# The last stage of a mixture-of-experts layer: expert outputs gathered in two parts, and the first weighting on ScalarE

## The chip, the core and the metric

The kernel runs on one core of a Trainium2 chip. The metric is the device time of one execution in microseconds (us). A profile of one execution gives the times of single instructions and transfers. Engines are called PE (TensorE), DVE (VectorE), ACT (ScalarE), POOL (GpSimd) and SP (SyncE).

## The reference

One layer serves two sequences, 128 prompt tokens and 256 sample tokens of width 2048, all float32. It has a token mixer (gated linear attention beside long convolutions) and then a mixture of experts. The change touches only the latter:

```python
def _moe(h, l, p):
    ...
    grp = jnp.argmax(lg, axis=-1)                      # one of 4 groups
    top_v, top_i = lax.top_k(jax.nn.softmax(le_sel, axis=-1), TOP_K_IN_GROUP)   # 2 of its 4 experts
    ids = grp[:, None] * EXP_PER_GROUP + top_i
    gates = jnp.sum(jax.nn.one_hot(ids, N_EXPERTS, dtype=f32) * (p_grp[:, None] * top_v)[..., None], axis=1)
    for e in range(N_EXPERTS):
        he = jax.nn.silu(t @ p['w_exp_gate'][l, e]) * (t @ p['w_exp_up'][l, e])
        out = out + gates[:, e:e + 1] * (he @ p['w_exp_down'][l, e]).astype(f32)

# in _layer, after it:
    x = x + gt2 * _rmsnorm(y, p['g_post_ffn'][l])
```

Each of the 384 tokens has two experts out of 16, so there are 768 pairs of a token and an expert. With the inputs used 44 of them are expert 15's, and none of the counts but two is above 64.

## The kernel before

The mixer and the router fill the time up to about 1250 us. The router ranks the 768 pairs and gives each a slot: an expert's pairs lie together, padded to blocks of 64 slots. `slot_i[:, r, t]` holds the slots of choice `r` of the 128 tokens of tile `t` (three tiles), `wpair` the two weights of each token. `tab_i` is a small table of numbers that all engines read into registers: the count of blocks `nblk`, and for each expert the number of the block after its last (`tab_i[..., MAXB + 2 + e]`, from `r_end`). The experts run in order, so the last block is the last expert's.

**The loop over blocks.** PE runs `expert_block(e, b)` (L706 to L739) once for each block. In this order it

- multiplies the block's token rows by the gate and up weights (L716, 64 matmuls),
- waits at L720 for `x_gathered >= b * 16 + 32`, and then turns the *next* block's rows into columns (`turn_rows`, L687, 16 transposes),
- waits for `he`, which ACT (silu, L1099) and DVE (product, L1488) make, turns it (L726),
- multiplies by the down weights (L736, 32 matmuls).

ACT and DVE evict the result (L1103, L1493) and ACT stores it to `y_slots` in DRAM with two DMAs (L1108, semaphore `y_stored`, 32 a block on top of 1).

**Weights.** SP loads six 2 MB pieces for each expert into nine places of 16 KB a partition (`MOE_SLOTS`), in turn; a load waits until PE has used the place (L813). The semaphore of place `i` is `w{i}`. The last piece is load number 95 and goes to place 5. Places 6, 7 and 8 take their last loads for expert 14, as loads 87 to 89.

**POOL.** Its queue is one list in program order. First its loop over `nblk + 1` fetches (L910 to L918): each waits until PE has turned the rows before it, loads 64 token numbers into `idx_i` (L913), waits for them and gathers those rows of `h_rows` into `hg` (L916; it adds 16 to `x_gathered`). PE's transposes of block 17 wait for the 19th fetch, number 18, though no block follows: all of its indices are beyond the table, and such rows are skipped. After its loop POOL waits for all stores (L920) and issues six gathers (L924), one for each tile and choice, 128 rows of 8 KB each.

**The tail.** DVE combines tile by tile (`combine`, L1497): the first row times its weight (L1501), plus the second row times its weight (L1504), times the gate of the modulation (L1510). ACT makes the sum of squares (L959) and the root (L965), DVE adds the residual (L1515), and SP stores the tile (L819).

Of the kernel before, what the change touches and what calls it, by code (L numbers as in the profile page):

```python
# [13 lines left out]
F32 = mybir.dt.float32  # L14
# [6 lines left out]
P = 128  # L21
# [22 lines left out]
RING = 3  # L44
BLK = 64
MAXB = NE + (2 * TOK - 2) // BLK
MAGIC = 1.5 * 2.0 ** 23
TWO_PI_HI = 6.28125
TWO_PI_LO = 2 * math.pi - TWO_PI_HI
# [84 lines left out]
def build(nc, T):  # L134

    ctx = ExitStack()
    with ctx:
        def sb(name, shape, dt=F32):
            return ctx.enter_context(nc.sbuf_tensor("s_" + name, shape, dt))
# [29 lines left out]
        tok_i = sb("tok_i", [P, NT], I32)  # L169
        tab_i = sb("tab_i", [P, MAXB + 2 + NE], I32)  # L170
        idx_i = sb("idx_i", [BLK, 1], I32)
        ident, tri = base[:, 0:P], base[:, P:2 * P]
        sel = base[:, 2 * P:4 * P].rearrange("p (c m) -> p c m", c=2)
        ps = ctx.enter_context(nc.psum_tensor("ps", [P, 8, NCOL], F32))
# [83 lines left out]
        he = at(AT_MOD + D, DE, rows=BLK)  # L258
        sg = at(AT_GAIN + 512, DE, rows=BLK)
        ysl = at(AT_GAIN + 1024, 2, NCOL)  # L260
        yga = [[region((2 * t + r) * D, D) for r in range(2)] for t in range(NT)]


        h_dram = nc.dram_tensor("h_rows", [TOK, D], F32).ap()
        y_dram = nc.dram_tensor("y_slots", [NE * BLK + 3 * DEC, D], F32).ap()
        tok_dram = nc.dram_tensor("tok_of_slot", [(MAXB + 1) * BLK, 1], I32).ap()

        x_rows = [T["x_prompt"][0], T["x_sample"][0, 0:P], T["x_sample"][0, P:2 * P]]
# [555 lines left out]
        def _(pool):  # L824
# [82 lines left out]
            pool.wait_ge(S("tables_ready"), 1)  # L907

            nblk = pool.value_load(tab_i[0:1, MAXB:MAXB + 1], min_val=NE, max_val=MAXB)
            with pool.Fori(0, nblk + 1) as b:  # L910
                pool.wait_ge(S("x_turns"), b * 2 + 1)
                pool.nop(nofuse=True)
                pool.dma_start(idx_i[:, :], tok_dram[bass.ds(b * BLK, BLK), :]).then_inc(S("idx_in"), 16)  # L913
                pool.wait_ge(S("idx_in"), b * 16 + 16)
                pool.nop(nofuse=True)
                pool.indirect_dma_start(out=hg, out_offset=None, in_=h_dram,  # L916
                                        in_offset=bass.IndirectOffsetOnAxis(ap=idx_i[:, :], axis=0),
                                        bounds_check=TOK - 1, oob_is_err=False).then_inc(S("x_gathered"), 16)  # L918

            pool.wait_ge(S("y_stored"), nblk * 32 + 1)  # L920
            pool.nop(nofuse=True)
            for t in range(NT):
                for r in range(2):
                    pool.indirect_dma_start(out=yga[t][r], out_offset=None, in_=y_dram,  # L924
                                            in_offset=bass.IndirectOffsetOnAxis(ap=slot_i[:, r, t:t + 1], axis=0)
                                            ).then_inc(S(f"y_gathered{t}{r}"), 16)


        @block.scalar
        def _(act):  # L930
# [165 lines left out]
            with act.Fori(0, nblk) as b:  # L1096
                act.wait_ge(S("used3"), b + 2)
                act.wait_ge(S("he_ready"), b + 1)
                A(sg, ps[BLK:2 * BLK, 0, :], ACT.Silu).then_inc(S("sg_ready"), 1)  # L1099
                turned(b * 2 + 4)  # L1100
                act.wait_ge(S("used5"), b + 2)
                act.wait_ge(S("y_stored"), b * 32 + 1)
                A(ysl[:, 0, :], ps[:, 4, :], ACT.Copy).then_inc(S("y_read_act"), 1)  # L1103
                act.wait_ge(S("y_read_act"), b + 2)
                act.wait_ge(S("y_read_dve"), b + 2)
                rows = y_dram[bass.ds(b * BLK, BLK), :].rearrange("r (a c n) -> r a c n", a=2, c=2)
                for c in range(2):
                    act.dma_start(rows[:, :, c, :], ysl[c * BLK:(c + 1) * BLK, :, :]).then_inc(S("y_stored"), 16)  # L1108
            for t in range(NT):
                act.wait_ge(S("y_added"), t + 1)  # L1110
                squares(yga[t][0], y_sb[:, 0, :], 32 + t)
                roots(32 + t, 1, D)
# [4 lines left out]
        def _(dve):  # L1117
# [283 lines left out]
            def step(ins, sem=None):  # L1401
                v.op(ins, sem)
                v.sync()
# [72 lines left out]
                                  ALU.add))  # L1476
            step(ve.tensor_scalar(r_tab[:, 0:MAXB], r_tab[:, 0:MAXB], float(NE - 1), None, ALU.min))
            v.op(ve.tensor_copy(tab_i[:, :], r_tab), S("tables_ready"))


            dve.wait_ge(S("tables_ready"), 1)
# [14 lines left out]

            def combine(t):  # L1497

                dve.wait_ge(S(f"y_gathered{t}0"), 16)
                y0, y1 = yga[t]  # L1500
                v.op(ve.tensor_scalar(y0, y0, wpair[:, 0, t:t + 1], None, ALU.mult))  # L1501
                v.sync()
                dve.wait_ge(S(f"y_gathered{t}1"), 16)
                v.op(ve.scalar_tensor_tensor(out=y0, in0=y1, scalar=wpair[:, 1, t:t + 1], in1=y0, op0=ALU.mult,  # L1504
                                             op1=ALU.add), S("y_added"))
                v.sync()
                if t < 2:
                    for j in range(4):
                        read(dve, f"gate1{j}{t}")
                v.op(ve.tensor_tensor(y1.rearrange("p (j n) -> p j n", j=4), y0.rearrange("p (j n) -> p j n", j=4),  # L1510
                                      ps[:, 4 * COND[t]:4 * COND[t] + 4, :], ALU.mult))
# [36 lines left out]
```

## Time and profile before

| | |
|---|---|
| median of 3 runs | 1816.5 us (1803.3 to 1820.69) |
| the profiled execution | 1822.51 us, of which the span is 1820.8 us |
| busy: PE, DVE, ACT, POOL | 1563.7, 376.1, 229.1, 82.4 us |
| DMA, mean over the span | 230 GB/s |
| the last 60 us: PE's last block's first matmul | 1748.14 us |
| PE's last down-projection matmul ends | 1777.7 us |
| first of the six gathers issued | 1783.38 us |
| DVE's last instruction ends | 1816.4 us |

How to read it: the engines' shares are means over stages with different limits. The change lies in the last 60 us, so what counts there is what each step waits for. Beside a wait it matters what stands behind the waiting instruction in the same engine's list. All DMAs that POOL issues go through one queue, those of SP and of ACT through one each; the page gives them as q0, q1 and q10.

### The profile page before, as it was taken

How to read it: one execution, taken by the hardware profiler on the slowest of the kernel's cores; microseconds unless marked ns; L12 is line 12 of the kernel's file. 1: busy time of each engine (PE TensorE's matmuls, PEld its weight loads, DVE VectorE, ACT ScalarE, POOL GpSimd, SP SyncE). 2: the span in 40 equal slices, each digit the busy share in tenths (PEclk: the TensorE clock that was granted, in tenths of full speed). 3: DMA queues.
4: the chain of work that ended last, by engine and by line, in shares of the span. 5: the costliest groups of instructions: out<-in, count | busy, mean ns of one | idle time of the engine just before them, and what ended most of it. 6: DMA issues, size and time to landing. Idle time of an engine off the chain costs nothing.

```text
span 1820.8 us, 14118 instructions
## 1 busy us (share of the span) xinstructions
PE 1563.7 (86%) x5712; PEld 714.3 (39%) x5712; DVE 376.1 (21%) x716; ACT 229.1 (13%) x370; POOL 82.4 (5%) x122
## 2 busy tenths in 40 slices
PE   3689989989999699999998999784998987899781
PEld 0244434434555354545454444362333332333230
DVE  0122300000213344445362000421000000000005
ACT  1203200100000101101012000210110110011011
POOL 4000000000000000000001000001000000000001
PEclk8889999999898699999898999756998998899995
DMA  9964544554615523424122221462999999999975
GB/s 350 421 254 180 218 170 171 231 190 180 236 46 220 191 98 139 162 93 145 46 93 73 93 93 51 180 271 80 404 404 359 404 401 399 411 393 399 395 330 219
DMA packets 67821, 418.30 MB, mean 230 GB/s; under 512 B 6827, under 2 KB 7068, under 8 KB 46036
## 3 DMA queue, kind: packets, MB, share of 16 engines
q1 hardware_dynamic: 55124, 375.69, 52.0%
q0 software_dynamic: 6496, 29.08, 4.9%
q10 hardware_dynamic: 6144, 12.71, 1.9%
q8 instruction: 44, 0.72, 0.2%
q14 instruction: 13, 0.11, 0.0%
HBM read 404.33 MB, written 23.08 MB: 235 GB/s over the span
## 4 chain that ended last, share of the span: by engine, by line
PE 70%; DMA 18%; DVE 5%; issue 4%; ACT 2%; POOL 0%; SPq 0%; ACTq 0%; POOLq 0%; DVEq 0%
PE ps L449 19%; PE ps L452 19%; PE ps L716 10%; DMA s_mem<-in_w_exp_gate 10%; PE ps L736 6%; DMA s_mem<-in_w_ada 4%; PE ps L378 3%; PE ps L554 3%; PE ps L614 2%; DMA s_mem<-in_w_in 2%; PE ps L566 2%; PE ps L420 1%; PE ps L522 1%; PE ps L503 1%; DMA s_mem<-in_hy_w 1%
## 5 line engine op out<-in xcount | busy, mean ns | idle before, releaser
L452 PE MATMUL ps<-s_mem 128*128 128x512 f32 x768 | 340.6, 605 | 14.9 <-DMA s_mem<-in_w_in 14.9
L449 PE MATMUL ps<-s_mem 128*128 128x384 f32 x1024 | 341.7, 495 | 5.6 <-DMA s_mem<-in_w_in 4.5
L716 PE MATMUL ps<-s_mem 128*64 128x512 f32 x1152 | 266.1, 620 | 34.1 <-DMA s_mem<-in_w_exp_gate 33.4
L449 PEld LDWEIGHTS ps<-s_mem 128*128 128x128 f32 x1024 | 197.5, 194 | 152.3 <-issue 16.0
L452 PEld LDWEIGHTS ps<-s_mem 128*128 128x128 f32 x768 | 147.8, 194 | 207.0 <-issue 189.4
L716 PEld LDWEIGHTS ps<-s_mem 128*64 128x64 f32 x1152 | 88.7, 143 | 208.4 <-issue 207.6
L736 PE MATMUL ps<-s_mem 128*64 128x512 f32 x576 | 148.4, 675 | 9.3 <-DVE s_mem L1490 9.3
L378 PE MATMUL ps<-s_mem,s_sT 128*32 128x512 f32 x768 | 103.3, 672 | 29.2 <-DMA s_mem<-in_w_ada 29.2
L736 PEld LDWEIGHTS ps<-s_mem 128*64 128x64 f32 x576 | 44.6, 154 | 99.9 <-issue 87.9
L1488 DVE TENSOR_TENSOR s_mem<-s_mem,ps 64x512 f32<-64x512 f32 x18 | 12.2, 679 | 338.8 <-ACT s_mem L1099 338.8
L984 ACT ACTIVATE s_mem<-ps 128x512 f32<-128x512 f32 (+1 forms) x69 | 39.0, 582 | 315.0 <-PE ps L452 187.7
L554 PE MATMUL ps<-s_mem 128*128 128x512 f32 x160 | 71.0, 599 | 3.1 <-ACT s_mem L984 3.1
L378 PEld LDWEIGHTS ps<-s_mem,s_sT 128*32 128x32 f32 x768 | 22.5, 117 | 99.2 <-issue 56.3
L1099 ACT ACT_TABLE_LOAD x18 | 23.1, 1283 | 287.2 <-PE ps L716 287.2
L687 PE MATMUL ps<-s_base,s_mem 64*128 64x64 f32 x304 | 37.5, 276 | 22.8 <-DMA s_mem<-h_rows,s_idx_i 22.8
L687 PEld LDWEIGHTS ps<-s_base,s_mem 64*128 64x128 f32 x304 | 34.9, 200 | 37.5 <-DMA s_mem<-h_rows,s_idx_i 22.9
L1036 ACT ACTIVATE s_mem<-ps,s_colB 128x384 f32<-128x384 f32 x24 | 16.1, 670 | 257.8 <-PE ps L449 257.8
L1159 DVE TENSOR_TENSOR s_mem<-s_mem,ps 128x512 f32<-128x512 f32 x6 | 4.1, 683 | 206.3 <-PE ps L378 206.3
L554 PEld LDWEIGHTS ps<-s_mem 128*128 128x128 f32 x160 | 29.5, 190 | 41.9 <-issue 35.0
L566 PE MATMUL ps<-s_mem,s_hdn 64*128 64x512 f32 x48 | 31.5, 806 | 14.8 <-DMA s_mem<-in_hy_w 12.7
L1493 DVE COPY s_mem<-ps 128x512 f32<-128x512 f32 x18 | 12.5, 692 | 152.0 <-PE ps L736 152.0
L1312 DVE RECIPROCAL s_mem<-ps 128x512 f32<-128x512 f32 x8 | 26.3, 3326 | 79.4 <-PE ps L575 79.4
(221 smaller groups left out, 964.3 us busy)
## 6 DMA issues: line engine op xcount, KB each, us to landing
s_mem<-in_w_ada SPq DMA_DIRECT2D x48, 2048.0 KB, 11.1
s_mem<-in_w_exp_up SPq DMA_DIRECT2D x32, 2048.0 KB, 30.7
s_mem<-in_w_exp_gate SPq DMA_DIRECT2D x32, 2048.0 KB, 26.6
s_mem<-in_w_exp_down SPq DMA_DIRECT2D x32, 2048.0 KB, 29.9
s_mem<-in_w_in SPq DMA_DIRECT2D x24, 2048.0 KB, 11.3
s_mem<-in_w_out SPq DMA_DIRECT2D x8, 2048.0 KB, 8.1
y_slots<-s_mem ACTq DMA_DIRECT2D x36, 256.0 KB, 12.2
h_rows<-s_mem SPq DMA_DIRECT2D x3, 1024.0 KB, 6.0
```

The source lines that it names most:

```text
L378: m = mm(ps[32 * j:32 * j + 32, bank, :], sT[:, k, :], w[:, n, :], start=(k == 0), stop=(k == KT - 1), skip_group_check=True)
L449: m = mm(ps[:, banks[m_], 0:TOK], v[:, k, m_ * P:(m_ + 1) * P], hT[:, kk, :], start=(kk == 0), stop=(kk == KT - 1))
L452: m = mm(ps[:, banks[m_], :], hT[:, kk, m_ * P:(m_ + 1) * P], v[:, k, :], start=(kk == 0), stop=(kk == KT - 1))
L554: m = mm(ps[:, bank, :], dft[:, FWD[t, rows], :], src(t), start=(t == tiles[0]), stop=(t == tiles[-1]))
L566: mm(ps[:, 4 + d, :], hdn[:, t * P:(t + 1) * P], w3[:, d, :], start=True, stop=True).then_inc(filled(f"f{ho}{t}{d}"), 1)
L614: m = mm(ps[:, t, :], dft[:, INV[r, t], :], Yb[:, r, :], start=(r == rows[0]), stop=(r == rows[-1]))
L687: m = tr(ps[:, 2 + i, q * BLK:(q + 1) * BLK], hg[:, k:D:KT], ident[0:BLK, 0:BLK])
L716: m = mm(ps[half, 0, :], hgT[:, kh * 8 + k, :], weights(e, 2 * kh + which)[:, k, :], start=(kh + k == 0), stop=(kh * 8 + k == KT - 1), ski ...
L736: m = mm(ps[half, 4 + n // 2, :], heT[:, 2 * kh + k, :], weights(e, 4 + kh)[:, k, n * NCOL:(n + 1) * NCOL], start=(kh + k == 0), stop=(kh ...
L984: a.op(A(dst, ps[:, b, 0:n], func), freed("act", key))
L1099: A(sg, ps[BLK:2 * BLK, 0, :], ACT.Silu).then_inc(S("sg_ready"), 1)
L1312: v.op(ve.reciprocal(Gs[:, 3 + s, :], ps[:, b, :]), freed("dve", f"norm{ho}{s}"))
```

## The change

Three things change.

- **POOL gathers twice.** Its loop of fetches is split at `last`, the end of expert 14's blocks, read from `tab_i` into a register. After fetch `last` it waits until the stores of all blocks before the last expert's are done, until the split tables are written, and until the last weight load has landed (`w5`). Then it issues six gathers with `early_i`. Then come the remaining fetches, `last + 1` to `nblk`. Then it waits for the early gathers and for all stores, and issues six gathers with `late_i`. The index tables are made so that the early ones skip the last expert's rows and the late ones skip all others (a skipped row's index is beyond the bound).
- **The destination of the rows** is places 6, 7 and 8 of the weights, in place of the region at the start of the arena.
- **The first weighting** (row one times its weight) moves from DVE to ACT, as `weigh(t)`, one tile ahead.

DVE makes the two index tables from `slot_i` in eight small operations.

```diff
@@ -44,6 +44,8 @@
 RING = 3
 BLK = 64
 MAXB = NE + (2 * TOK - 2) // BLK
+Y_ROWS = NE * BLK + 3 * DEC
+NO_ROW = 4096
 MAGIC = 1.5 * 2.0 ** 23
 TWO_PI_HI = 6.28125
 TWO_PI_LO = 2 * math.pi - TWO_PI_HI
@@ -169,6 +171,9 @@
         tok_i = sb("tok_i", [P, NT], I32)
         tab_i = sb("tab_i", [P, MAXB + 2 + NE], I32)
         idx_i = sb("idx_i", [BLK, 1], I32)
+        early_i = sb("early_i", [P, 2 * NT], I32)
+        late_i = sb("late_i", [P, 2 * NT], I32)
+        split = sb("split", [P, 3 * 2 * NT + 1])
         ident, tri = base[:, 0:P], base[:, P:2 * P]
         sel = base[:, 2 * P:4 * P].rearrange("p (c m) -> p c m", c=2)
         ps = ctx.enter_context(nc.psum_tensor("ps", [P, 8, NCOL], F32))
@@ -258,11 +263,12 @@
         he = at(AT_MOD + D, DE, rows=BLK)
         sg = at(AT_GAIN + 512, DE, rows=BLK)
         ysl = at(AT_GAIN + 1024, 2, NCOL)
-        yga = [[region((2 * t + r) * D, D) for r in range(2)] for t in range(NT)]
+        yga_at = [MOE_SLOTS[i] + o for i in (6, 7, 8) for o in (0, D)]
+        yga = [[at(yga_at[2 * t + r], D) for r in range(2)] for t in range(NT)]


         h_dram = nc.dram_tensor("h_rows", [TOK, D], F32).ap()
-        y_dram = nc.dram_tensor("y_slots", [NE * BLK + 3 * DEC, D], F32).ap()
+        y_dram = nc.dram_tensor("y_slots", [Y_ROWS, D], F32).ap()
         tok_dram = nc.dram_tensor("tok_of_slot", [(MAXB + 1) * BLK, 1], I32).ap()

         x_rows = [T["x_prompt"][0], T["x_sample"][0, 0:P], T["x_sample"][0, P:2 * P]]
@@ -907,7 +913,9 @@
             pool.wait_ge(S("tables_ready"), 1)

             nblk = pool.value_load(tab_i[0:1, MAXB:MAXB + 1], min_val=NE, max_val=MAXB)
-            with pool.Fori(0, nblk + 1) as b:
+            last = pool.value_load(tab_i[0:1, MAXB + 2 + NE - 2:MAXB + 2 + NE - 1], min_val=1, max_val=MAXB)
+
+            def fetch(b):
                 pool.wait_ge(S("x_turns"), b * 2 + 1)
                 pool.nop(nofuse=True)
                 pool.dma_start(idx_i[:, :], tok_dram[bass.ds(b * BLK, BLK), :]).then_inc(S("idx_in"), 16)
@@ -917,13 +925,31 @@
                                         in_offset=bass.IndirectOffsetOnAxis(ap=idx_i[:, :], axis=0),
                                         bounds_check=TOK - 1, oob_is_err=False).then_inc(S("x_gathered"), 16)

+            def gather_y(index):
+                for t in range(NT):
+                    for r in range(2):
+                        at_ = r * NT + t
+                        pool.indirect_dma_start(out=yga[t][r], out_offset=None, in_=y_dram,
+                                                in_offset=bass.IndirectOffsetOnAxis(ap=index[:, at_:at_ + 1], axis=0),
+                                                bounds_check=Y_ROWS - 1, oob_is_err=False
+                                                ).then_inc(S(f"y_gathered{t}{r}"), 16)
+
+            with pool.Fori(0, last + 1) as b:
+                fetch(b)
+            pool.wait_ge(S("y_stored"), last * 32 + 1)
+            pool.nop(nofuse=True)
+            pool.wait_ge(S("slots_split"), 1)
+            i = LOADS_A_EXPERT * NE - 1
+            pool.wait_ge(S(f"w{i % len(MOE_SLOTS)}"), 16 * (i // len(MOE_SLOTS) + 1))
+            gather_y(early_i)
+            with pool.Fori(last + 1, nblk + 1) as b:
+                fetch(b)
+            for t in range(NT):
+                for r in range(2):
+                    pool.wait_ge(S(f"y_gathered{t}{r}"), 16)
             pool.wait_ge(S("y_stored"), nblk * 32 + 1)
             pool.nop(nofuse=True)
-            for t in range(NT):
-                for r in range(2):
-                    pool.indirect_dma_start(out=yga[t][r], out_offset=None, in_=y_dram,
-                                            in_offset=bass.IndirectOffsetOnAxis(ap=slot_i[:, r, t:t + 1], axis=0)
-                                            ).then_inc(S(f"y_gathered{t}{r}"), 16)
+            gather_y(late_i)


         @block.scalar
@@ -1106,7 +1132,14 @@
                 rows = y_dram[bass.ds(b * BLK, BLK), :].rearrange("r (a c n) -> r a c n", a=2, c=2)
                 for c in range(2):
                     act.dma_start(rows[:, :, c, :], ysl[c * BLK:(c + 1) * BLK, :, :]).then_inc(S("y_stored"), 16)
+            def weigh(t):
+                act.wait_ge(S(f"y_gathered{t}0"), 32)
+                a.op(A(yga[t][0], yga[t][0], ACT.Copy, scale=wpair[:, 0, t:t + 1]), S("y_weighed"))
+
+            weigh(0)
             for t in range(NT):
+                if t + 1 < NT:
+                    weigh(t + 1)
                 act.wait_ge(S("y_added"), t + 1)
                 squares(yga[t][0], y_sb[:, 0, :], 32 + t)
                 roots(32 + t, 1, D)
@@ -1476,6 +1509,16 @@
                                   ALU.add))
             step(ve.tensor_scalar(r_tab[:, 0:MAXB], r_tab[:, 0:MAXB], float(NE - 1), None, ALU.min))
             v.op(ve.tensor_copy(tab_i[:, :], r_tab), S("tables_ready"))
+            n = 2 * NT
+            slot_f, is_late, moved, cut = split[:, 0:n], split[:, n:2 * n], split[:, 2 * n:3 * n], split[:, 3 * n:3 * n + 1]
+            v.op(ve.tensor_scalar(cut, r_end[:, NE - 2:NE - 1], float(BLK), None, ALU.mult))
+            step(ve.tensor_copy(slot_f, slot_i.rearrange("p r t -> p (r t)")))
+            step(ve.tensor_scalar(is_late, slot_f, cut, float(NO_ROW), ALU.is_ge, ALU.mult))
+            step(ve.tensor_tensor(moved, slot_f, is_late, ALU.add))
+            step(ve.tensor_copy(early_i[:, :], moved))
+            step(ve.tensor_tensor(moved, slot_f, is_late, ALU.subtract))
+            step(ve.tensor_scalar(moved, moved, float(NO_ROW), None, ALU.add))
+            step(ve.tensor_copy(late_i[:, :], moved), S("slots_split"))


             dve.wait_ge(S("tables_ready"), 1)
@@ -1496,11 +1539,9 @@

             def combine(t):

-                dve.wait_ge(S(f"y_gathered{t}0"), 16)
+                dve.wait_ge(S("y_weighed"), t + 1)
                 y0, y1 = yga[t]
-                v.op(ve.tensor_scalar(y0, y0, wpair[:, 0, t:t + 1], None, ALU.mult))
-                v.sync()
-                dve.wait_ge(S(f"y_gathered{t}1"), 16)
+                dve.wait_ge(S(f"y_gathered{t}1"), 32)
                 v.op(ve.scalar_tensor_tensor(out=y0, in0=y1, scalar=wpair[:, 1, t:t + 1], in1=y0, op0=ALU.mult,
                                              op1=ALU.add), S("y_added"))
                 v.sync()
```

On POOL, from its loop of fetches to the end, the list before is as follows (an ISA row is a register, branch or wait instruction; "waits" names semaphores):

```order
L910 UNCONDITIONAL_BRANCH
L910 ISA
L913 ISA [waits x_turns]
L913 DMA s_idx_i<-tok_of_slot 64x1
L914 ISA
L916 DMA s_mem<-h_rows,s_idx_i 64x2048 [waits idx_in]
L910 ISA
L910 COMPARE_AND_BRANCH
L920 ISA
L924 DMA s_mem<-y_slots,s_slot_i 128x2048 [waits y_stored]
L924 DMA s_mem<-y_slots,s_slot_i 128x2048 x5
```

And with the change, from the end of its first loop of fetches:

```order
L937 COMPARE_AND_BRANCH
L939 ISA
L932 DMA s_mem<-y_slots,s_early_i 128x2048 [waits y_stored,w5,slots_split]
L932 DMA s_mem<-y_slots,s_early_i 128x2048 x5
L945 ISA
L945 UNCONDITIONAL_BRANCH
L945 ISA
L921 ISA [waits x_turns]
L921 DMA s_idx_i<-tok_of_slot 64x1
L922 ISA
L924 DMA s_mem<-h_rows,s_idx_i 64x2048 [waits idx_in]
```

The last fetches now stand behind three waits and six gathers. On PE nothing has moved; in `expert_block` it has, with the change as before:

```order
L726 ISA
L693 MATMUL ps<-s_base,s_mem 128x64 [waits x_gathered]
L693 MATMUL ps<-s_base,s_mem 128x64 x15
L729 REGISTER_ALU
L732 MATMUL ps<-s_base,s_mem 128x64 [waits he_ready]
L732 MATMUL ps<-s_base,s_mem 128x64 x3
L742 MATMUL ps<-s_mem 64x512 [waits y_read_dve,w4,y_read_act,he_turned]
```

These are the transposes of the next block's rows, those of `he`, and the first down matmuls, with the wait for the fetch ahead of all three. In the tail ACT now begins with

```order
L1137 ACTIVATE s_mem<-s_mem,s_wpair 128x2048 [waits y_gathered00]
L1137 ACTIVATE s_mem<-s_mem,s_wpair 128x2048 [waits y_gathered10]
L985 ACTIVATE s_mem,s_stat<-s_mem 128x2048 [waits y_weighed,y_added]
L991 ACT_TABLE_LOAD
L991 ACTIVATE s_stat<-s_stat 128x1 [waits act_step]
L1137 ACTIVATE s_mem<-s_mem,s_wpair 128x2048 [waits y_gathered20]
```

where only the squares, the table load and the root stood; the number of table loads is the same.

## Rows read from the trace of the kernel before

**Rows 1.** the page's DMA issues: engine, op, count, KB, us to landing.

```profile
y_slots<-s_mem ACTq DMA_DIRECT2D x36, 256.0 KB, 12.2
```

**Rows 2.** the chain of waits from 1600 us: start, us, what.

```profile
1768.96 8.81 PE ps L736 x32
...
1779.51 3.08 DMA y_slots<-s_mem
...
1792.54 2.36 DVE s_mem L1504
...
1797.21 1.21 DVE s_mem L1501
```

**Rows 3.** timeline of POOL: start, us, instruction [idle before <-releaser].

```profile
1248.40 0.57 POOL L913 DMA_DIRECT2D s_idx_i<-tok_of_slot  x1 [3.91 <-issue]
...
1251.48 0.97 POOL L916 DMA_INDIRECT s_mem<-h_rows,s_idx_i  x1 [2.50 <-DMA s_idx_i<-tok_of_slot]
...
1746.19 0.95 POOL L916 DMA_INDIRECT s_mem<-h_rows,s_idx_i  x1 [5.88 <-DMA s_idx_i<-tok_of_slot]
...
1783.38 0.98 POOL L924 DMA_INDIRECT s_mem<-y_slots,s_slot_i  x1 [36.24 <-DMA y_slots<-s_mem]
...
1789.66 1.55 POOL L924 DMA_INDIRECT s_mem<-y_slots,s_slot_i  x1 [0.31 <-issue]
```

**Rows 4.** instructions on h_rows, 1738 to 1760: fetch 18.

```profile
L916 POOL DMA_INDIRECT s_mem<-h_rows,s_idx_i x1: 949/949/949, 1746.2 to 1746.2; - x1
...
DMA to landing us min/median/max: 7.5/7.5/7.5
```

**Rows 5.** timeline of the last block, 1762 to 1784.

```profile
1764.86 1.97 PE L687 MATMUL ps<-s_base,s_mem 64*128 64x64 f32 x16
...
1767.78 0.66 PE L726 MATMUL ps<-s_base,s_mem 64*128 64x64 f32 x4 [0.95 <-DVE s_mem L1488]
...
1768.48 0.42 DVE L1490 COPY s_mem<-ps 128x256 f32<-128x256 f32 x1 [0.84 <-PE ps L726]
```

**Rows 6.** instructions on y_slots, 1748 to 1760: block 16's stores.

```profile
L1108 ACTq DMA_DIRECT2D y_slots<-s_mem x2: 543/544/544, 1749.4 to 1750.1; - x2
...
DMA to landing us min/median/max: 9.8/12.7/15.7
```

**Rows 7.** instructions on in_w_exp_down, 1735 to 1752: last load.

```profile
L788 SPq DMA_DIRECT2D s_mem<-in_w_exp_down x1: 327/327/327, 1737.5 to 1737.5; - x1
...
DMA to landing us min/median/max: 30.6/30.6/30.6
```

**Rows 8.** source line 924, the six gathers: issue to landing.

```profile
DMA to landing us min/median/max: 5.6/9.6/12.6
```

**Rows 9.** on s_idx_i, 1247 to 1253: index load (min), gather (max).

```profile
DMA to landing us min/median/max: 2.2/3.5/4.7
```

**Rows 10.** on tok_of_slot, 1243 to 1247: the last two scatters.

```profile
DMA to landing us min/median/max: 3.1/3.2/3.3
```

**Rows 11.** the chain of waits: 64 matmuls of block 0, of block 14.

```profile
1258.95 17.02 PE ps L716 x64
...
1656.37 13.78 PE ps L716 x64
```

**Rows 12.** windows: us, PE PEld DVE ACT POOL, PEclk, DMA, GB/s.

```profile
1770.00:1774.00 4.00, 4.00 (x14) 1.13 (x12) 0.00 (x0) 0.00 (x0) 0.00 (x0) 0.57 0.00 0
```

**Rows 13.** timeline of ACT from 1785: a pass over 128x2048.

```profile
1794.93 1.91 ACT L959 ACTIVATE s_mem<-s_mem 128x2048 f32<-128x2048 f32 x1 [16.46 <-DVE s_mem L1504]
```

**Rows 14.** the chain from 1226: DVE's cast, POOL's table read.

```profile
1236.63 0.18 DVE s_slot_i L1469
...
1246.70 0.50 POOLq L909
...
1247.52 0.03 POOLq L910
```

## The prediction, made before the change ran

> **What bounds the kernel now.** I read the page first: PE is busy for 86% of the span, but the last thing to end is a tail after it. Then I read the chain of waits over the last 60 us, because the change touches little else. It runs: down projection of the last block (8.8 us, from 1768.96), eviction, store of the block's rows to DRAM (landed at 1782.6), six gathers, then DVE's combining from 1792.54 to 1816.41 [rows 2]. From there to the end of the span are 4.4 us of output store. So the tail from PE's last down-projection matmul (1777.77) is worth about 43 us, and the change wants a part of it.
>
> The second thing to read is who needs POOL. POOL does two jobs in one program order: it fetches the token rows of block b (an index load, then a gather), and afterwards it gathers the results. There are 18 blocks (36 stores, two a block [rows 1]) and POOL makes 19 fetches, one more than blocks. Block b on PE transposes the rows of block b+1 in its middle, and waits for fetch b+1 to do so (`x_gathered >= 16b+32`), also in the last block, number 17, whose next block does not exist. In the profile that wait costs nothing: fetch 18 is issued at 1746.19 [rows 3] and lands 7.5 us later [rows 4], at 1753.7, while PE starts the transposes at 1764.86 [rows 5]. 11 us are to spare.
>
> **The change, part by part.**
>
> (a) *When the early gathers start.* Expert 15 has one block here, so `last` is 17. POOL now makes fetches 0 to 17 only, then waits for the stores of block 16, for the last weight load, and issues the six early gathers; **fetch 18 comes behind them**. The stores of block 16 are issued at 1749.4 and 1750.1 and the later lands after up to 15.7 us, at 1765 or so [rows 6]. The last weight load is issued at 1737.5 and lands 30.6 us later, at 1768.1 [rows 7]. That one ends last. From a landing to POOL's first gather the profile shows 0.79 us (1782.59 to 1783.38), so the first early gather is issued at 1768.9.
>
> (b) *How long they hold the queue.* Six gathers take 7.83 us to issue (1783.38 to 1789.66+1.55) [rows 3], so POOL is at fetch 18 at about 1777.5, where it was at 1739.8 before. But the six gathers land one behind another: the first 5.6 us after its issue, the last 12.6 us after its own, that is at 1802.26, 18.9 us after the first issue [rows 8]. With the reference's routing 44 of the 768 row pairs belong to expert 15 and are left out early, 94.3% remain: 5.3 + 0.943 x 13.3 = 17.8 us, so the last lands at 1786.7. The index load of fetch 18 is issued in the same queue behind them; I take 1787.0 for its landing. Against the row stands the Trainium skill, "DMA: Bandwidth & Descriptors", section on the anatomy of one DMA: it fits a transfer that GpSimd issues as 2.0 us plus the bytes at 436 GB/s. The six early gathers would by that take an estimated 15.6 us in place of 17.8, and the whole sum would be some 2 us smaller; the six full ones before should then have taken 16.4 us, and they took 18.9, so the row decides.
>
> (c) *Fetch 18 and the new wait.* From the landing of an index load to the gather's issue: 1250.6 to 1251.48, 0.86 us [rows 3, 9]. The gather of fetch 18 finds only indices beyond the table and moves no rows. No row shows this in an idle DMA: below stands the bare index load, 2.2 us, above it a full gather of 64 rows with idle queues, 4.7 us [rows 9], and far above the same empty gather among weight loads, 7.5 us [rows 4]. The nearest is an indirect transfer of next to no bytes with idle queues, the scatter of token numbers, 3.1 to 3.3 us [rows 10]. I take 3.1. It lands at 1787.0 + 0.9 + 3.1 = 1791.0. PE transposes then instead of at 1764.86: **26.2 us late**. Behind PE's wait stand the transposes of `he`, the down projection, and with them ACT's and DVE's evictions and the store. `he` itself has long been ready, so from the start of the first transposes to the down projection are 2.05 + 0.1 + 0.7 + 0.5 = 3.4 us, where it was 4.1: the down projection starts 25.5 us late.
>
> (d) *The clock.* PE will have been idle for 26 us. After the idle 22.8 us ahead of the first block PE restarted at 1256.2 with transposes, and the next 64 matmuls, from 1258.95, took 17.02 us against 13.78 us later on [rows 11]. One takes 13.78/64 = 0.215 us at 2.4 GHz and twice that at 1.2, so the 3.24 us more are 15 slow ones, up to 1265.4: 9.2 us after the restart. Restarting at 1791.0 the down projection (from 1794.4) has 5.8 us of that, 13.5 matmuls at 0.43, and the other 18.5 of its 32 at 0.215: 9.8 us. Before it was not at full clock either: 8.8 us, with a granted clock of 0.57 from 1770 to 1774 [rows 12]. So +1.1 us; the bounds are 6.9 (all at 2.4 GHz) and 13.8 (all at 1.2). The end of PE is 26.6 us later, and the store, untouched, too.
>
> (e) *The tail.* It gets shorter. Late gathers move only 44 rows; I price their landing like the scatter's, 3.1 us after issue (bounds 2.2 and the 5.6 of a full one). DVE's first real combination started 9.16 us after the first gather's issue (1783.38 to 1792.54); now first rows land after 3.1, ACT weighs them in about 2.0 (its 128x2048 pass takes 1.91 [rows 13]), and row two is there at 1.3 + 3.1: 5.2, a gain of 4.0 us. From there DVE went on for 23.9 us, with two more first weightings of 1.3 us each on its path [rows 2]; those are on ACT now, whose weighting of tile 1 and 2 falls beside DVE's two passes of 2.3 us. Gain 2.6. No table load is added, since the copy comes under the loop's last table. Together **-6.6 us**.
>
> (f) *The head of the stage.* POOL reads one more table entry before its first fetch, for which PE waits: the one it reads now takes 0.8 us from 1246.70 [rows 14]. +0.8, or nothing at best. DVE's eight small operations (0.2 us each, as its 128x3 cast is [rows 14]) run while PE waits for that fetch, and DVE is first needed in the loop behind the 17.02 us of matmuls in rows 11. Nothing, then; without that cover they would cost 1.6 us.
>
> Sum: 26.6 - 6.6 + 0.8 = **+20.8 us**. Against the profiled execution's 1822.5 us that is 1843.3; against the median of the runs shown, 1816.5, which is 6 us lower, 1837.3. The forecast is 1837 us, 1.1% slower. Its own range: the empty gather at 2.2 or 7.5 (-0.9, +4.4), the clock (-2.9, +4.0), late landings (-0.9, +2.5): 1831 to 1847.
>
> **Rivals.**
> 1. *Fetch 18 isn't held by the gathers' data.* The index load is tiny, and if it slips past them it lands 2.2 us after its issue: gather at 1780.6, landed 1783.8, PE 7.2 us less late. +13.6: 1830. Against it: the six landings, each about 2.4 us after the one before. For it: with the weight loads of another queue in full flow an index load still comes in within some 6 us (5.88 of idle time ahead of the gather of fetch 18 [rows 3]). The skill's page named above, section on queues, rings and completion order, says that a DMA engine takes the descriptors of one ring in order and that a semaphore increment lands after all earlier writes of its engine; by that the rival has no place, and no row here has an index load behind gathers. Chance 0.15.
> 2. *The stall is longer.* Fetch 18 takes 7.5 us as in rows 4 and the down projection stays at 1.2 GHz: +8 on the forecast, 1845. For it only that both were seen, though in other surroundings. Chance 0.1.
> 3. *Not slower: the early gathers really run beside the last expert.* Place: PE's wait ahead of the transposes in block 17. If 19 fetches were issued ahead of the early gathers, PE would keep its times, the late rows would land at about 1787 behind the early ones, and DVE would start at 1789.0 instead of 1792.5: -3.5 - 2.6 + 0.8 = -5.3, 1811, within 1%. It decides from the point where fetch 18 lands before 1764.9. Against it: the order on POOL and the count in PE's wait, both plain in the program; it would need `last` to be 18, and a fetch count that ends with the loop. Chance 0.05.
>
> The forecast has 0.7. About 1% (18 us) is what a measurement of this kernel tells from no change. The forecast's lower part, rival 1 and rival 3 fall within it, and so would a pair of medians that are off by a few us, since the three runs shown lie 17 us apart. Slower by over 1%: 0.6. Within: 0.37. Faster by over 1%: 0.03, since no case reaches -18. The range for 8 in 10 takes rival 1 with its lower bounds and the upper end of the forecast: 1823 to 1848.
>
> **What would show it.** The six early gathers start at about 1769 (a). The gather of fetch 18 starts at 1788, after them, not at 1746 (b). PE has an idle stretch of some 25 us before its last 16 transposes, released by a DMA of `h_rows` (c); it is about 19 if rival 1 holds, none if rival 3 does. The last down projection takes near 10 us (d). DVE's first combination comes 5 us after the first late gather, and 21 us before DVE's end (e). The prediction is wrong at its root if PE's idle time there is under 10 us; it is wrong in size if the stall is there and the tail is shorter or longer than 26 us from first late gather to DVE's end.

## The result, and the profile after

The changed kernel takes 1840.3 us (median of 4 runs, 1836.5 to 1844.3) against 1818.0 us for the kernel before. The ratio is 1.0121, with a 95% interval of 1.0090 to 1.0151: slower by about 22 us, and the interval reaches from 16 to 27. The forecast was +20.8 us, 1837, range 1823 to 1848. One execution of e2 below (1846.4 us) and one of e3 (2394.4 us) had a lower granted TensorE clock than the others of their kernels, 0.87 and 0.63, and are left out of the ratios.

The profiled execution of the changed kernel took 1836.5 us, with a span of 1834.7. It is on the quick side, and the stretch up to the last block ran 4 us faster than in the profile before. That is scatter: in the ten traces of this document the point named next lies anywhere from 1759.5 to 1767.3. So I compare from one point on, called the zero point below: the end of the last block's gate and up matmuls, the last thing on PE ahead of the wait. It lies at 1764.93 in the profile before and at 1760.90 after. From there to the end of the span were 55.9 us and are now 73.8.

First the timeline of POOL, which answers to [rows 3]. Columns: start us, duration us, instruction, and in brackets the idle time before it with what ended it.

```profile
1764.96 1.03 POOL L932 DMA_INDIRECT s_mem<-y_slots,s_early_i  x1 [59.01 <-DMA s_mem<-in_w_exp_down]
...
1771.50 0.99 POOL L932 DMA_INDIRECT s_mem<-y_slots,s_early_i  x1 [0.30 <-issue]
1772.49 0.59 POOL L921 DMA_DIRECT2D s_idx_i<-tok_of_slot  x1
1784.88 0.96 POOL L924 DMA_INDIRECT s_mem<-h_rows,s_idx_i  x1 [11.79 <-DMA s_idx_i<-tok_of_slot]
```

The six early gathers start 4.06 us behind the zero point, released by the last weight load. The fetch of the block that doesn't exist comes right behind them, and **its index load of 256 bytes takes 11.57 us to land**, where the same load took 2.2 us with idle queues [rows 9]. Then what PE, ACT and DVE did, in answer to [rows 5] (the same columns):

```profile
1753.81 7.09 PE L722 MATMUL ps<-s_mem 128*64 128x512 f32 x32 [2.78 <-DMA s_mem<-in_w_exp_gate]
...
1762.92 0.68 DVE L1531 TENSOR_TENSOR s_mem<-s_mem,ps 64x512 f32<-64x512 f32 x1 [17.93 <-ACT s_mem L1125]
...
1787.04 2.00 PE L693 MATMUL ps<-s_base,s_mem 64*128 64x64 f32 x16 [26.15 <-DMA s_mem<-h_rows,s_idx_i]
...
1790.04 8.62 PE L742 MATMUL ps<-s_mem 128*64 128x512 f32 x32 [0.52 <-DVE s_mem L1533]
```

`he` is ready at 1763.6, and PE stands idle for 26.15 us, up to 1787.04, until the rows of the block that doesn't exist are in. The chain of waits (start, us, what) shows the piece that PE waited for, and the tail, in answer to [rows 2]:

```profile
1772.49 11.57 DMA s_idx_i<-tok_of_slot
...
1784.88 2.03 DMA s_mem<-h_rows,s_idx_i
...
1790.04 8.65 PE ps L742 x32
...
1800.42 3.08 DMA y_slots<-s_mem
...
1804.34 2.75 DMA s_mem<-y_slots,s_late_i
...
1807.11 2.01 ACT s_mem L1137
...
1809.14 2.36 DVE s_mem L1545
...
1828.01 2.35 DVE s_mem L1556
```

The tail is indeed shorter: the first late rows land after 2.75 us, ACT weighs them, and DVE's first combination starts 4.80 us after the first late gather (before: 9.16). From there to DVE's end are 21.2 us (before: 23.9).

### The profile page after: what moved, and what is told of

Same layout as the page of the kernel before. It is cut to its first block, busy times and chain, and to the rows that moved or that the text cites. A ratio compares the mean times of both kernels' runs of the same rounds, so it can differ in the third digit from the quotient of the medians.

```text
span 1834.7 us, 14155 instructions
## 1 busy us (share of the span) xinstructions
PE 1557.2 (85%) x5712; PEld 710.9 (39%) x5712; DVE 373.3 (20%) x721; ACT 235.3 (13%) x373; POOL 90.0 (5%) x128
## 4 chain that ended last, share of the span: by engine, by line
PE 70%; DMA 18%; DVE 5%; issue 4%; ACT 2%; POOL 1%; SPq 0%; POOLq 0%; ACTq 0%; DVEq 0%
PE ps L458 19%; PE ps L455 18%; PE ps L722 10%; DMA s_mem<-in_w_exp_gate 8%; PE ps L742 6%; DMA s_mem<-in_w_ada 4%; PE ps L384 3%; PE ps L560 3%; DMA s_mem<-in_w_in 2%; PE ps L620 2%; DMA s_mem<-in_w_exp_down 2%; PE ps L572 2%; PE ps L426 1%; PE ps L528 1%; DMA s_idx_i<-tok_of_slot 1%
## 5 line engine op out<-in xcount | busy, mean ns | idle before, releaser
L455 PEld LDWEIGHTS ps<-s_mem 128*128 128x128 f32 x1024 | 196.6, 193 | 151.2 <-issue 15.1
L384 PE MATMUL ps<-s_mem,s_sT 128*32 128x512 f32 x768 | 103.8, 673 | 29.7 <-DMA s_mem<-in_w_ada 29.7
L1062 ACT ACTIVATE s_mem<-ps,s_colB 128x384 f32<-128x384 f32 x24 | 16.1, 671 | 258.3 <-PE ps L455 258.3
L560 PEld LDWEIGHTS ps<-s_mem 128*128 128x128 f32 x160 | 29.5, 190 | 41.9 <-issue 35.0
L1536 DVE COPY s_mem<-ps 128x512 f32<-128x512 f32 x18 | 12.4, 691 | 151.1 <-PE ps L742 151.1
## 6 DMA issues: line engine op xcount, KB each, us to landing
s_mem<-in_w_exp_gate SPq DMA_DIRECT2D x32, 2048.0 KB, 26.2
y_slots<-s_mem ACTq DMA_DIRECT2D x36, 256.0 KB, 12.4
```

The lines of the kernel that those rows point to most:

```text
L384: m = mm(ps[32 * j:32 * j + 32, bank, :], sT[:, k, :], w[:, n, :], start=(k == 0), stop=(k == KT - 1), skip_group_check=True)
L455: m = mm(ps[:, banks[m_], 0:TOK], v[:, k, m_ * P:(m_ + 1) * P], hT[:, kk, :], start=(kk == 0), stop=(kk == KT - 1))
L560: m = mm(ps[:, bank, :], dft[:, FWD[t, rows], :], src(t), start=(t == tiles[0]), stop=(t == tiles[-1]))
```

## The experiments

All distances below are read from the timelines, one trace for each kernel, in us from the end of the last gate and up matmul to: the start of the down projection, its length, the issue of the last block's store, the first late gather (before: the first gather), DVE's first combination, DVE's end, and the end of the span. The first row is the kernel before. The ratio is that to the kernel before, with its 95% interval.

| kernel | down starts | lasts | store | gather | combination | DVE's end | span's end | ratio |
|---|---|---|---|---|---|---|---|---|
| before | 4.0 | 8.8 | 13.9 | 18.5 | 27.6 | 51.5 | 55.9 | 1 |
| the change | 29.1 | 8.6 | 38.8 | 43.4 | 48.2 | 69.5 | 73.8 | 1.0121 (1.0090 to 1.0151) |
| e1, fetches first | 4.1 | 9.9 | 15.1 | 24.8 | 29.5 | 50.8 | 55.1 | 0.9992 (0.9962 to 1.0022) |
| e2, weighting only | 4.0 | 8.8 | 13.9 | 18.5 | 27.8 | 49.5 | 53.8 | 0.9978 (0.9952 to 1.0003) |
| e3, empty early gathers | 19.8 | 10.0 | 30.9 | 35.5 | 44.9 | 66.4 | 70.8 | 1.0080 (1.0045 to 1.0114) |
| e4, e1 and a wait for each | 4.0 | 8.8 | 13.9 | 25.0 | 29.7 | 50.9 | 55.3 | 1.0001 (0.9976 to 1.0025) |
| e5, e4 without `w5` | 4.0 | 8.5 | 13.6 | 24.8 | 29.4 | 50.6 | 55.1 | 1.0014 (0.9988 to 1.0041) |
| e6, e4 with two tiles early | 4.1 | 9.9 | 15.1 | 20.2 | 25.0 | 46.2 | 50.6 | 0.9961 (0.9934 to 0.9988) |
| e7, e6 without `w5` | 4.0 | 8.8 | 13.9 | 18.5 | 23.2 | 44.4 | 48.8 | 0.9969 (0.9945 to 0.9992) |
| e8, e4 with one tile early | 4.0 | 8.8 | 13.9 | 18.5 | 23.2 | 46.8 | 51.2 | 0.9974 (0.9949 to 0.9999) |

### e1: all fetches ahead of the early gathers

```diff
-            with pool.Fori(0, last + 1) as b:
+            with pool.Fori(0, nblk + 1) as b:
                 fetch(b)
...
             gather_y(early_i)
-            with pool.Fori(last + 1, nblk + 1) as b:
-                fetch(b)
```

> The changed kernel with all 19 fetches ahead of the early gathers. Theory (the whole loss is PE's wait for fetch 18, which stands behind the early gathers on POOL): the idle stretch ahead of the last 16 transposes goes from 26.1 us to under 1 us, and PE's last matmul ends as far behind the last gate/up matmul as before (12.8 us, against 37.8 in the changed kernel). POOL's late gathers then wait for the early ones, which end 18.9 us after their first issue, about 5 us after the last store has landed, so DVE's first combination starts about 0.7 us later than before and the tail behind it is 2.6 us shorter: -2 us in all, ratio 0.999. Rival (the early gathers' traffic itself disturbs the last block, whatever stands where on POOL): PE stays idle for 10 us or more there, or the last store lands much later than 3.1 us after its issue, and the ratio stays at 1.006 or more.

This undoes one thing, the place of the last fetch on POOL, and nothing else. The loss is gone: 0.9992. Timeline of POOL and PE (columns as above):

```profile
1741.17 0.95 POOL L924 DMA_INDIRECT s_mem<-h_rows,s_idx_i  x1 [5.85 <-DMA s_idx_i<-tok_of_slot]
...
1754.01 7.09 PE L722 MATMUL ps<-s_mem 128*64 128x512 f32 x32 [2.12 <-DMA s_mem<-in_w_exp_gate]
1761.03 1.97 PE L693 MATMUL ps<-s_base,s_mem 64*128 64x64 f32 x16
...
1765.18 9.94 PE L742 MATMUL ps<-s_mem 128*64 128x512 f32 x32 [0.52 <-DVE s_mem L1531]
1765.22 1.04 POOL L932 DMA_INDIRECT s_mem<-y_slots,s_early_i  x1 [23.10 <-DMA s_mem<-in_w_exp_down]
...
1785.91 0.99 POOL L932 DMA_INDIRECT s_mem<-y_slots,s_late_i  x1 [13.13 <-DMA y_slots<-s_mem]
```

The transposes at 1761.03 have no wait before them, and the early gathers run beside the down projection as the change meant them to. So the cause of the loss is shown: PE's wait for a fetch that stood behind the early gathers. But the tail gave back less than I had thought for this case, since the late gathers start 24.8 us from the zero point and not 18.5. Part of the rival came true as well: the traffic does disturb one thing, the last store. (The down projection's 9.9 us are the clock's doing, as point (d) below shows.) The instructions on `y_slots` from 1776 to 1778, with issue to landing:

```profile
L1132 ACTq DMA_DIRECT2D y_slots<-s_mem x2: 544/544/544, 1776.2 to 1776.9; - x2
...
DMA to landing us min/median/max: 7.6/7.9/8.2
```

They took 3.1 us before. The first half lands at 1783.8 (1776.2 + 7.6) and the second at 1785.1 (1776.9 + 8.2). The last early gather, issued at 1771.8, lands 12.7 us later (the instructions on `s_early_i`, of which the last line is the maximum), at 1784.5, between the two:

```profile
L932 POOL DMA_INDIRECT s_mem<-y_slots,s_early_i x6: 993/998/1044, 1765.2 to 1771.8; - x6
...
DMA to landing us min/median/max: 8.4/9.8/12.7
```

The stores stand in ACT's queue, not in POOL's, and yet they need 7.6 and 8.2 us while the gathers' data is in flight. The Trainium skill ("DMA: Bandwidth & Descriptors", queues, rings and completion order) has a sentence that bears on it: a completion increment lands only after every earlier write from the same DMA engine, across its queues. The landings show no more than a delay, for they do not come in a fixed order: in e4 both halves of the store land before the last early gather does. Whether it is that rule or the sharing of the engines' time isn't told apart here.

### e2: the weighting alone

```diff
+            def weigh(t):
+                act.wait_ge(S(f"y_gathered{t}0"), 16)
+                a.op(A(yga[t][0], yga[t][0], ACT.Copy, scale=wpair[:, 0, t:t + 1]), S("y_weighed"))
...
-                dve.wait_ge(S(f"y_gathered{t}0"), 16)
+                dve.wait_ge(S("y_weighed"), t + 1)
                 y0, y1 = yga[t]
-                v.op(ve.tensor_scalar(y0, y0, wpair[:, 0, t:t + 1], None, ALU.mult))
-                v.sync()
```

> The kernel before with nothing changed but the first weighting, which ACT does. Theory (the moved weighting gives what it took on DVE's path): the first combination still waits for the second gather, landed 7.8 us after its issue, so nothing is gained there; two weightings of 1.3 us leave DVE's path, -2.6 us, ratio 0.9986; from DVE's first combination to its end 21.2 us instead of 23.9. Rival (ACT becomes the bound, since its weighting takes 2.0 us and stands ahead of the squares): 23.9 us or more stay, ratio 1.000 or above.

The profile has the gain where it was expected: the first combination starts as late as before, since it waits for the second gather, and then DVE needs 21.6 us where it needed 23.9. Of the 0.4 us over the expected 21.2, 0.32 are a wait for the rows of tile 1. So the gain is shown in the trace. The ratio 0.9978 agrees with it (0.9986 was expected), but its interval reaches 1.0003, and the times alone would not show a gain.

### e3: early gathers that move nothing

```diff
+            step(ve.tensor_scalar(moved, slot_f, float(NO_ROW), None, ALU.add))
             step(ve.tensor_copy(early_i[:, :], moved))
-            step(ve.tensor_tensor(moved, slot_f, is_late, ALU.subtract))
-            step(ve.tensor_scalar(moved, moved, float(NO_ROW), None, ALU.add))
-            step(ve.tensor_copy(late_i[:, :], moved), S("slots_split"))
+            step(ve.tensor_copy(late_i[:, :], slot_f), S("slots_split"))
```

> The changed kernel with an early index table that skips every row, and a late one that gathers them all: six early gathers are still issued ahead of fetch 18, but move no data. Theory (fetch 18 waits for the data of the gathers in the queue, not for their issue): the index load of fetch 18 lands about 2.2 us after its issue instead of 11.6, PE's idle stretch shrinks from 26.1 to about 16.7 us, which are the wait for the last weight load, 7.8 us of issues and the fetch itself; the tail is that of six full gathers. Against before about +13 us, ratio 1.007. Rival (the making of six gathers' descriptors holds what follows, whatever they move): the index load still takes near 11 us, PE is idle for about 26 us and the ratio is 1.014 or more.

```profile
1772.19 0.99 POOL L932 DMA_INDIRECT s_mem<-y_slots,s_early_i  x1 [0.30 <-issue]
1773.18 0.59 POOL L921 DMA_DIRECT2D s_idx_i<-tok_of_slot  x1
1776.18 0.96 POOL L924 DMA_INDIRECT s_mem<-h_rows,s_idx_i  x1 [2.41 <-DMA s_idx_i<-tok_of_slot]
1778.35 2.00 PE L693 MATMUL ps<-s_base,s_mem 64*128 64x64 f32 x16 [16.84 <-DMA s_mem<-h_rows,s_idx_i]
```

With six issues and no data ahead of it the index load lands in 2.2 us. PE's idle time goes from 26.15 to 16.84 us. The ratio is 1.0080, as expected, and the rival is out. So the stall has two parts: 9.3 us are the early gathers' data, and the other 16.8 are the wait for the last weight load (4.1), six issues (7.5), and the fetch itself (5.2). Even six early gathers without data cost more there than the 7.0 us that the tail gave back. That the data stands in the same queue as the index load isn't shown to matter: the store of e1, in another queue, was held up too.

### e4 and e5: shorter waits for the late gathers

e4 is e1 with each late gather waiting for its own early one. e5 also drops the wait for the last weight load.

```diff
-            def gather_y(index):
+            def gather_y(index, landed=0):
...
+                        if landed:
+                            pool.wait_ge(S(f"y_gathered{t}{r}"), landed)
...
-            for t in range(NT):
-                for r in range(2):
-                    pool.wait_ge(S(f"y_gathered{t}{r}"), 16)
             pool.wait_ge(S("y_stored"), nblk * 32 + 1)
             pool.nop(nofuse=True)
-            gather_y(late_i)
+            gather_y(late_i, landed=16)
# e5 also:
-            i = LOADS_A_EXPERT * NE - 1
-            pool.wait_ge(S(f"w{i % len(MOE_SLOTS)}"), 16 * (i // len(MOE_SLOTS) + 1))
```

> As the first of these kernels (all fetches first), and each late gather waits only for the early gather into the same rows, not for all six. Theory (late rows queue behind the early data in POOL's one queue, but no longer behind a wait): the first late gather is issued 0.8 us after the last store has landed, 1783.4 on the time scale of before, but lands only with the end of the early data, 4 to 5 us after its issue instead of 2.7; DVE's first combination starts about 2.4 us earlier than before and the tail is 2.6 shorter: -5 us, ratio 0.997. Rival (late gathers pass the early data, or the early data has ended by then): first landing 2.7 us after issue, -7 us or more, ratio 0.996 or less.

The step I expected to gain gained nothing. POOL's idle time before the late gathers is ended by the store in e1 and in e4: the wait for all early rows was not the last to end in e1 (1784.5, against 1785.1 for the store). The expectation had left out that the store would be late again, and it was. The two halves of e4's store, then its early gathers:

```profile
L1131 ACTq DMA_DIRECT2D y_slots<-s_mem x2: 543/543/543, 1774.9 to 1775.6; - x2
...
DMA to landing us min/median/max: 7.7/8.6/9.6
...
L934 POOL DMA_INDIRECT s_mem<-y_slots,s_early_i x6: 989/998/1044, 1765.1 to 1771.7; - x6
...
DMA to landing us min/median/max: 9.8/12.1/14.5
```

The halves land at 1782.6 and 1785.2, the last early gather at 1786.2. The store is slow here as in e1, but it does not wait for the end of the gathers.

> As the kernel with all fetches first and a wait for each row's own early gather, but the early gathers no longer wait for the last weight load; they start when the stores of block 16 have landed. Theory (the last block's store lands only when the early gathers' data has drained, as the run with all fetches first showed, 8 us after its issue instead of 3.1): the early data starts and ends about 3 us earlier, the store lands 2 to 3 us earlier, and the gain over before grows from about 2 to 4 or 5 us, ratio 0.9975. Rival (weights and gathers share a full DMA, so the last weights come later by what the gathers take): PE waits in its last down projection and the ratio is 1.000 or more.

Neither theory holds. PE did not wait (its down projection starts at 4.0 and takes 8.5 us), so the rival has the ratio right and the cause wrong, and nothing was gained (1.0014, and the late gathers at 24.8). The theory rested on a reading of e1, that the store lands only when the gathers' data has drained, which the landings of e1 and e4 don't bear out. The early gathers started at 3.0 and not at 4.1, only 1 us earlier, since the store of block 16 now opened them, and that too lands late among the weights (10.0 and 16.1 us):

```profile
L1129 ACTq DMA_DIRECT2D y_slots<-s_mem x2: 543/544/544, 1751.2 to 1751.9; - x2
...
DMA to landing us min/median/max: 10.0/13.1/16.1
```

### e6, e7, e8: fewer rows early

e6 is e4 with the rows of tiles 0 and 1 gathered early, those of tile 2 all at the end; e7 is e6 without the wait for the last weight load; e8 is e4 with tile 0 alone.

```diff
-            gather_y(early_i)
+            gather_y(early_i, tiles=range(2))
...
-            gather_y(late_i, landed=16)
+            gather_y(late_i, landed=16, tiles=range(2))
+            for t in range(2, NT):
+                for r in range(2):
+                    pool.indirect_dma_start(out=yga[t][r], out_offset=None, in_=y_dram,
+                                            in_offset=bass.IndirectOffsetOnAxis(ap=slot_i[:, r, t:t + 1], axis=0)
+                                            ).then_inc(S(f"y_gathered{t}{r}"), 16)
...
-                act.wait_ge(S(f"y_gathered{t}0"), 32)
+                act.wait_ge(S(f"y_gathered{t}0"), 32 if t < 2 else 16)
...
-                dve.wait_ge(S(f"y_gathered{t}1"), 32)
+                dve.wait_ge(S(f"y_gathered{t}1"), 32 if t < 2 else 16)
```

> As the kernel with all fetches first and a wait for each row's own early gather, but only the rows of tiles 0 and 1 are gathered early, those of tile 2 all at the end. Theory (early data in flight delays the last store): four gathers have landed about 13.5 us after the first issue, before or as the last store is made, so the store lands about 3.5 us after its issue, DVE's first combination starts 4.8 us after the first late gather, and tile 2 comes in time: -6 us against before, ratio 0.9967. Rival (the store is late for another reason): it lands 7 us or more after its issue as with six, and the ratio is 0.999 or more.

The last early gather is issued at 1771.0 and lands by 1781.0. The store is issued at 1778.0 and 1778.7 and lands 3.4 to 3.6 us later:

```profile
1771.03 1.01 POOL L934 DMA_INDIRECT s_mem<-y_slots,s_early_i  x1 [0.30 <-issue]
...
1783.19 0.99 POOL L934 DMA_INDIRECT s_mem<-y_slots,s_late_i  x1 [11.15 <-DMA y_slots<-s_mem]
...
1795.88 2.00 ACT L1139 ACTIVATE s_mem<-s_mem,s_wpair 128x2048 f32<-128x2048 f32 x1 [1.02 <-DMA s_mem<-y_slots,s_slot_i]
```

ACT waits 1 us for tile 2's rows, which costs DVE nothing: from its first combination to its end are 21.2 us. At 0.9961, with an interval of 0.9934 to 0.9988, this version is faster than the kernel before, and faster than the changed one by 1.6% (0.9961/1.0121). It is the lowest of eight ratios, but the traces of e6, e7 and e8 all point the same way: their spans end 4.7 to 7.1 us sooner than before, counted from the zero point.

> As the kernel with tiles 0 and 1 early, without the wait for the last weight load. Theory: nothing of the early data is left at the last store, which lands 3.1 us after its issue; -7 us against before, ratio 0.996, the least this tail allows. Rival (the last weights are late instead): PE waits in its last down projection by what is gained, ratio as with the wait or worse.

The profile of e7 has the shortest tail of all, 48.8 us, with a store that lands in 3.1 us. In the runs it cannot be told from e6.

> As the kernel with tiles 0 and 1 early, but tile 0 alone early. Theory: the store lands 3.1 us after its issue and the first combination comes 4.8 us after the first late gather, but tile 1's full rows land about 2 us after DVE could use them: -5 us against before, ratio 0.9974. Rival (the end is bound by the count of late bytes): DVE waits 5 us or more between tiles, ratio 0.999 or above.

```profile
1790.54 2.35 DVE L1547 SCALAR_TENSOR_TENSOR s_mem<-s_mem,s_wpair 128x2048 f32<-128x2048 f32 x1 [9.59 <-ACT s_mem L1139]
1792.92 2.29 DVE L1553 TENSOR_TENSOR s_mem<-s_mem,ps 128x2048 f32<-128x2048 f32 x1
1797.47 2.35 DVE L1547 SCALAR_TENSOR_TENSOR s_mem<-s_mem,s_wpair 128x2048 f32<-128x2048 f32 x1 [2.26 <-DMA s_mem<-y_slots,s_slot_i]
```

With one tile early DVE waits 2.26 us for tile 1, as expected, and the ratio is 0.9974. In the traces two tiles are better than one (DVE's end at 44.4 in e7 against 46.8, with the same down projection) and than three (50.9 in e4): as much as fits between the last weights and the last store. The times do not tell one tile from two.

## Why the prediction was right, point by point

The mechanism and its size held. Two terms of (b) and (c) were off by about 1 us each and cancel, which is luck; the clock in (d) was off by 1.3 us and is most of what the sum has too much.

- **(a) Start of the early gathers.** 4.0 us from the zero point expected, 4.06 measured, opened by the last weight load. Right.
- **(b) The queue.** I expected the six early gathers to take 17.8 us from first issue to last landing, since 5.7% of the rows are left out. They took 18.9 (1764.96 to 1771.50 + 12.4), the time of the six full ones before, and the index load landed 1 us later than forecast. By the fit of the Trainium skill ("DMA: Bandwidth & Descriptors", anatomy of one DMA) it would have been an estimated 15.6; the trace sides against it more than I had. A slip stands in the issue of fetch 18: 1768.9 + 7.83 is 1776.7 and not 1777.5. The forecast doesn't use it, but rival 1 does, and is 0.8 us too high by it.
- **(c) Fetch and stall.** The empty gather landed in 2.0 us, not 3.1, which takes back that 1 us. PE's idle time is 26.15 us where 26.2 was forecast, and e1 shows that without this wait the loss is gone. From the first transposes to the down projection were 3.0 us, not 3.4, so that it started 25.1 us late and not 25.5.
- **(d) The clock.** This step failed in size: +1.1 us forecast, -0.2 measured. Windows (us, busy time of PE, PEld, DVE, ACT and POOL, granted clock, DMA) of the changed kernel, of e3 and of the kernel before:

```profile
1787.04:1793.00 5.96, 5.44 (x28) 3.29 (x30) 0.42 (x1) 1.19 (x2) 0.00 (x0) 0.50 0.00 0
1793.25:1798.66 5.41, 5.41 (x26) 1.54 (x22) 0.00 (x0) 0.00 (x0) 0.00 (x0) 1.00 0.00 0
...
1778.35:1787.00 8.65, 8.13 (x34) 4.01 (x36) 0.42 (x1) 1.19 (x2) 0.00 (x0) 0.50 0.00 0
...
1770.25:1773.50 3.25, 3.25 (x10) 0.98 (x8) 0.00 (x0) 0.00 (x0) 0.00 (x0) 0.50 0.00 0
```

  After 26 us of idle time PE did restart at a granted clock of 0.50 (1.2 GHz), as forecast, but had 2.4 GHz back 6.1 us later, not 9.2; in e3, after 16.8 us of idle time, it took 8.9. So 3.1 us of the changed kernel's down projection ran at 1.2 GHz and 5.9 us of e3's. The kernel before had 3.4 us at 1.2 GHz in the middle of its own, and e1 and e6, where PE had no such wait, 5.8. A matmul takes twice as long there, so 2.4 us more at 1.2 GHz are 1.2 us more in all, which is what lies between 8.8 and 9.9 or 10.0. What counts is how much of the down projection falls into such a stretch, and that came to about the same before and after the change. I had carried the price over from one stretch, block 0; the long idle time lengthened no down projection beyond those of e1 and e6.
- **(e) The tail.** -6.6 forecast, -7.0 measured: DVE's end is 26.0 us behind the first late gather, before 33.0. The split was right too (first combination after 4.8 us, 5.2 forecast; 21.2 us from there, 21.3 forecast), and e2 shows the second part by itself.
- **(f) The head.** 0.8 us forecast for the second table read. From POOL's first table read to its first index load are 2.25 us (1241.83 to 1244.08), before 1.70 (1246.70 to 1248.40), so 0.6, within the bounds.

From the zero point the traces differ by 17.9 us; with 0.6 at the head that is 18.5, against 20.8 forecast: 1.3 us of the difference are (d), 0.4 the start of the down projection, 0.4 the tail and 0.2 the head. The times say 22 (16 to 27), which includes 18.5. The forecast's own bounds, added up, end at 1848 and not at 1847.

The two rivals on the stall fell: the index load did not slip past the gathers' data (11.57 us, and 2.2 in e3), and the fetch was not slow. The rival that ends not slower was right in that the order on POOL decides, as e1 did what it described, but its number was wrong. I gave it -5.3 us, of which -6.1 lie behind the zero point. There e1's span ends 0.8 us sooner; its down projection of 9.9 us in place of 8.8 hides 1.1 more, so -1.9. I had missed that the last store, though in another queue, takes 7.6 to 8.2 us to land and not 3.1 while the early gathers' data is in flight. That POOL waits for all early gathers before the late ones, which I had missed too, cost nothing.

## What to carry to other kernels

Before work is put ahead of something in an engine's program order, look for who waits for what is behind it; here it was a fetch whose rows nobody uses, kept only because a loop makes one turn too many, and it cost 25 us. A transfer that is moved into a quiet stretch should have drained, or nearly so, before the next short transfer on the critical path is issued, whichever of the queues tried here that one is in; so move as much as fits, and not all. Split such a change: the weighting alone shortens the span by 2 us in its trace (its times don't tell it from nothing), and that was buried under the other half.

## What the runs showed of the hardware

- A 256 KB store of ACT's queue landed in 3.1 us with quiet DMA engines, in 3.4 to 3.6 us when the last of four gathers landed 3 us after the store's issue (e6), in 7.6 to 9.6 us with six gathers of POOL's queue ahead of it (e1, e4, e5), and in 9.7 to 16.1 us among weight loads of SP's queue.
- An indirect gather whose 128 or 64 indices are all beyond the bound lands 2.0 to 2.1 us after its issue with otherwise idle queues, and POOL still takes 0.96 to 1.03 us to issue it and 0.30 until the next.
- Six gathers of 128 rows of 8 KB took 18.9 us from first issue to last landing with 5.7% of the rows skipped (the change), and 18.9 to 19.2 us with none (before, e2, e3). With a store among them the former took 19.3 to 21.1 us (e1, e4, e5).
- The fifth of the last six gathers took 2.7 to 2.8 us to issue instead of 0.99 in the change, e1 and e4 to e8, where two to six gathers with data had gone ahead, and not in e2 and e3. What causes it was not tried. It cost nothing here, since its rows are needed last.
